# Attention key pages laid out with the head dimension first: no turning of key pages, one ring of key buffers

## The reference, cut to what matters

```
s = einsum('bqngd,bqknd->bqngk', qg, kg) * Dh ** -0.5     # 8 query heads on 2 key heads
s = where(valid, s, -inf);  p = softmax(s)
y = einsum('bqngk,bqknd->bqngd', p, vg)
```

## Time and profile before

| | |
|---|---|
| runs | 1834.33, 1837.55, 1839.07 us, median 1837.55 |
| profiled execution, first to last instruction | 1838.1 us |
| its whole time | not shown apart; its span lies within the three runs' times |
| PE busy | 1747.2 us, 95% |
| DVE, ACT, POOL busy | 979.2, 612.0, 413.3 us |
| instructions | 26511 |

### The profile page before, as it was taken

How to read it: one execution, slowest core, us unless ns; L and a number is a source line. 1 busy time by engine, 2 the same in 40 slices (tenths; PEclk the granted TensorE clock), 3 DMA queues, 4 the chain that set the end, 5 groups by cost and what they waited for, 6 DMA issues and landing times. The chain is left out here.

```text
span 1838.1 us, 26511 instructions
## 1 busy us (share of the span) xinstructions
PE 1747.2 (95%) x9413; PEld 1351.6 (74%) x9413; DVE 979.2 (53%) x2279; ACT 612.0 (33%) x1271; POOL 413.3 (22%) x643
## 2 busy tenths in 40 slices
PE   6999999999999998998999999999999679999999
PEld 5666788777887887886876566887777456777887
DVE  5412644233677555212442568888879665774111
ACT  3110332111122113101211346888745445553010
POOL 4301221100143352000342001211005455420000
PEclk9999999999999999999999999999999899999999
DMA  6433343544556467122222121334344774242231
GB/s 215 131 111 117 120 122 100 162 140 148 181 180 186 128 226 300 76 96 70 82 68 75 47 75 65 117 99 146 126 142 116 252 229 156 90 127 66 105 121 46
DMA packets 134765, 237.10 MB, mean 129 GB/s; under 512 B 28550, under 2 KB 61222, under 8 KB 134634
## 3 DMA queue, kind: packets, MB, share of 16 engines
q1 hardware_dynamic: 111066, 172.48, 29.2%
q0 software_dynamic: 17184, 55.85, 9.6%
q10 hardware_dynamic: 6384, 7.08, 1.1%
HBM read 169.12 MB, written 66.17 MB: 128 GB/s over the span
## 5 line engine op out<-in xcount | busy, mean ns | idle before, releaser
L1282 PE MATMUL ring_acc<-ring_w_hi,layer_xT_hi 128*128 128x512 f32 x640 | 260.8, 407 | 0.2 <-PE all_banks L1432 0.2
L1284 PE MATMUL ring_acc<-ring_w_hi,layer_xT_lo 128*128 128x512 f32 x640 | 249.9, 391 | 0.0
L1283 PE MATMUL ring_acc<-ring_w_lo,layer_xT_hi 128*128 128x512 f32 x640 | 249.7, 390 | 0.0
L2869 PE MATMUL front_acc<-front_w_hi,front_xT_hi 128*128 128x512 f32 x520 | 217.1, 417 | 8.3 <-DVE front_w_lo L3415 6.5
L2871 PE MATMUL front_acc<-front_w_hi,front_xT_lo 128*128 128x512 f32 x520 | 204.5, 393 | 0.0
L2870 PE MATMUL front_acc<-front_w_lo,front_xT_hi 128*128 128x512 f32 x520 | 204.2, 393 | 0.0
L1282 PEld LDWEIGHTS ring_acc<-ring_w_hi,layer_xT_hi 128*128 128x128 f32 x640 | 120.3, 188 | 29.5 <-issue 6.6
L1284 PEld LDWEIGHTS ring_acc<-ring_w_hi,layer_xT_lo 128*128 128x128 f32 x640 | 120.1, 188 | 26.2
L1283 PEld LDWEIGHTS ring_acc<-ring_w_lo,layer_xT_hi 128*128 128x128 f32 x640 | 120.4, 188 | 25.3 <-issue 2.6
L3195 ACT ACTIVATE front_index_rows<-odd_bias,front_candidate,front_minus_sign 128x1024 bf16<-128x1024 f32 (+1 forms) x124 | 132.5, 1075 | 7.2 <-DVE front_candidate L3509 7.2
L2869 PEld LDWEIGHTS front_acc<-front_w_hi,front_xT_hi 128*128 128x128 f32 x520 | 97.9, 188 | 40.3 <-issue 11.8
(11 more groups left out here) (718 smaller groups left out, 3594.6 us busy)
## 6 DMA issues: line engine op xcount, KB each, us to landing
all_w<-in_w_even POOLq DMA_DIRECT2D x80, 256.0 KB, 3.8
h_even<-layer_st SPq DMA_DIRECT2D x79, 256.0 KB, 2.2
all_w<-in_w_odd POOLq DMA_DIRECT2D x61, 256.0 KB, 3.4
h_odd<-front_st SPq DMA_DIRECT2D x55, 256.0 KB, 2.1
layer_scratch<-h_even SPq DMA_DIRECT2D x46, 256.0 KB, 3.0
all_scratch<-in_w_mem SPq DMA_DIRECT2D x32, 256.0 KB, 3.8
all_scratch<-h_even SPq DMA_DIRECT2D x32, 256.0 KB, 3.6
all_scratch<-x SPq DMA_DIRECT2D x14, 512.0 KB, 3.8
```

The lines of the kernel that those rows point to most:

```text
L1282: T.matmul(out[0:rows, :], xh[:, kk, to], wh[:, r, :], start=(kk == 0), stop=False)
L1283: T.matmul(out[0:rows, :], xh[:, kk, to], wl[:, r, :], start=False, stop=False)
L1284: ins = T.matmul(out[0:rows, :], xl[:, kk, to], wh[:, r, :], start=False, stop=(kk == KC - 1))
L2869: T.matmul(out[0:rows, :], xh[:, k, to], wh[:, r, :], start=(k == 0), stop=False, skip_group_check=True)
```

## The change

The host lays the cache out as `cache_attn_kT[layer, page, kv_head, head_dim, position]`, so that a page arrives with the head dimension on the partitions: 128 partitions with 2 runs of 128 positions, 512 bytes each. The transposes, both copies, the ring skT and the semaphores ktr, kca and kcd go. There is one set of key buffers: units 0 and 1 in the four raw tiles (loaded by SP in the front stage, with one DMA for each page and key head, 16 of 64 KB), and eight places for the units from 2 on (`wide`, `place`); units 10 to 15 take the places of units 2 to 7 again and wait for the scores of the group that used them (`keys_free`). Units 2 and 3 are no longer loaded in the front stage. In the back stage step s loads unit s + 1: unit 2 in step 1, unit 3 in step 2, and so on, with AHEAD = 3. The scores wait for their own group's pages.

```diff
@@ layer1_front, SP @@
             def first_keys(u, to, n_pool):
                 for p in range(4):
                     page = sp.value_load(c.page_ids[...], min_val=0, max_val=n_pool - 1)
-                    src = a["cache_attn_k"][0, bass.ds(page, 1)].rearrange("o s h d -> (o s) (h d)")
-                    sp.dma_start(to[p], src).then_inc(kp_in, 16)
+                    src = a["cache_attn_kT"][0, bass.ds(page, 1)].rearrange("o n d s -> d (o n) s")
+                    for n in range(KVH):
+                        sp.dma_start(to[n][:, P * p:P * p + P], src[:, n, :]).then_inc(kp_in, 16)
...
                 sp.wait_ge(vmix, NB)
-                for u in (2, 3):
-                    first_keys(u, [Q[:, EARLY_KEYS + ...] for p in range(4)], n_pool)
+                for _ in range(2):
                     yield
@@ layer1_back @@
+        place = lambda u: u if u < 10 else u - 8
+        wide = {r: (... four places of WH and WL for r in 2 to 9 ...)}
+        keys_of = lambda u, n: c.raw[KVH * u + n] if u < 2 else wide[place(u)][:, n, :]
...
+        def key_page(eng, u, p):
+            at = PAGES * seq_of(u) + 4 * unit(u)[1] + p
+            page = eng.value_load(c.page_ids[0:1, at:at + 1], ...)
+            return a["cache_attn_kT"][0, bass.ds(page, 1)].rearrange("o n d s -> d (o n) s")
+
+        def keys_free(eng, u):
+            if place(u) != u:
+                eng.wait_ge(sc2, place(u) // 4 + 1)
@@ SP @@
             def load_k(u):
-                if u >= KRING:
-                    sp.wait_ge(ktr, 2 * (u - KRING + 1))
+                keys_free(sp, u)
                 for p in range(4 - len(by_pool(u))):
-                    sp.dma_start(kp[r][p], src).then_inc(kp_in[r], 16)
+                    sp.dma_start(wide[place(u)][:, :, P * p:P * p + P], key_page(sp, u, p)).then_inc(kp_in[u // 4], 16)
...
-                for u in range(UNITS + 7):
-                    if u + KRING < UNITS:
-                        load_k(u + KRING)
+                load_k(2)
+                yield
+                for u in range(UNITS + 6):
+                    if u + AHEAD < UNITS:
+                        load_k(u + AHEAD)
@@ POOL: the same for load_last_k @@
@@ PE @@
-            def turned(u):
-                ...
-                for n, (bank, copied) in enumerate(((bankX, kca), (bankZ, kcd))):
-                    pe.wait_ge(copied, u)
-                    for p in range(4):
-                        ins = T.transpose(bank[:, P * p:P * p + P], kp[r][p][:, HD * n:HD * n + HD], c.ident[:, :])
-                    ins.then_inc(ktr, 1)
             def smp_scores(m):
-                pe.wait_ge(kca, 4 * m + 4)
-                pe.wait_ge(kcd, 4 * m + 4)
                 if m == 0:
                     pe.wait_ge(qcp, 6)
+                late = range(max(2, 4 * m), 4 * m + 4)
+                pe.wait_ge(kp_in[m], 16 * sum(4 - len(by_pool(u)) for u in late))
+                pe.wait_ge(kq_in[m], 16 * sum(len(by_pool(u)) for u in late))
                 pe.wait_ge(ye, m)
@@ ACT and DVE: one copy for each unit goes, the steps stay @@
-                    A(skT[u % TRING][:, 0, :], bankX, ACT.Copy).then_inc(kca, 1)
-                        V.tensor_copy(skT[u % TRING][:, 1, :], bankZ).then_inc(kcd, 1)
@@ host @@
+    r["cache_attn_kT"] = turned(f["cache_attn_k"], 0, 1, 3, 4, 2)
```

More of the change, by code:

```diff
@@ L2353, in front_plan @@
     return plan, amid
-EARLY_KEYS = 2640
+MEM_PAGES = 2640
 def layer1_front(nc, c, a, o):
@@ L2434, in layer1_front @@
         qTm = S[:, 4096:5120].rearrange("p (h b q) -> p h b q", h=NH, b=NB)
-        cc = [Q[:, EARLY_KEYS + 1024 * u:EARLY_KEYS + 1024 * u + 1024].rearrange("p (m n) -> p m n", m=MC) for u in range(2)]
+        cc = [Q[:, MEM_PAGES + 1024 * u:MEM_PAGES + 1024 * u + 1024].rearrange("p (m n) -> p m n", m=MC) for u in range(2)]
         mss, mx, tot = ([s.sb(f"{n}{u}", [P, NH]) for u in range(2)] for n in ("mem_rstd", "mem_max", "mem_total"))
@@ L2646, in loads_qk @@
                 sp.dma_start(c.rope[0:SMP, TILES], a["rope"][SEQ:TOK]).then_inc(qk_par, 16)
-                n_pool = a["cache_attn_k"].shape[1]
+                n_pool = a["cache_attn_kT"].shape[1]
                 yield
                 sp.wait_ge(vmix, NB)
-                for u in (2, 3):
-                    first_keys(u, [Q[:, EARLY_KEYS + 1024 * (u - 2) + 256 * p:EARLY_KEYS + 1024 * (u - 2) + 256 * p + 256] for p in range(4)], n_pool)
+                for _ in range(2):
                     yield
@@ L2659, in loads_qk @@
                 for u in range(2):
-                    first_keys(u, [c.key_page(u, p) for p in range(4)], n_pool)
+                    first_keys(u, [c.raw[KVH * u + n] for n in range(KVH)], n_pool)
                 yield
@@ L4108, in load_last_k @@
             def load_last_k(u):
-                r, (gr, hf, _) = u % KRING, unit(u)
-                if u >= KRING:
-                    pool.wait_ge(ktr, 2 * (u - KRING + 1))
+                keys_free(pool, u)
                 for p in by_pool(u):
[L4113 to L4116, removed]
+                    pool.dma_start(wide[place(u)][:, :, P * p:P * p + P], key_page(pool, u, p)).then_inc(kq_in[u // 4], 16)
             def load_v(b, pages):
@@ L4122, in smps @@
             def smps():
-                for u in range(UNITS + 7):
-                    if u + KRING < UNITS:
-                        load_last_k(u + KRING)
+                load_last_k(2)
+                yield
+                for u in range(UNITS + 6):
+                    if u + AHEAD < UNITS:
+                        load_last_k(u + AHEAD)
                     if 12 <= u < 16:
@@ L4198, in smp_scores @@
                         u, e = 4 * m + q, slice(32 * q, 32 * q + 32)
-                        ins = T.matmul(bankY[e, :], qz[:, n, seq_of(u), e], skT[u % TRING][:, n, :], start=(n == 0), stop=(n == 1),
+                        ins = T.matmul(bankY[e, :], qz[:, n, seq_of(u), e], keys_of(u, n), start=(n == 0), stop=(n == 1),
                                        skip_group_check=True)
@@ L4407, in smps @@
             def smps():
-                for u in range(UNITS):
-                    act.wait_ge(ktr, 2 * u + 1)
-                    if u >= TRING:
-                        act.wait_ge(sc2, (u - TRING) // 4 + 1)
-                    A(skT[u % TRING][:, 0, :], bankX, ACT.Copy).then_inc(kca, 1)
+                for _ in range(UNITS):
                     yield
```

45 lines of the change are left out of this document (13 added, 32 removed).

## The result

The changed kernel takes 1840.71 us (median of 19 runs, 1836.37 to 1847.37) against 1837.52 us of the kernel before beside it (19 runs, 1834.07 to 1841.41). The ratio is 1.0020, 95% interval 1.0011 to 1.0029: 3.2 us slower by the medians, 3.7 by the ratio. The loss is just to be told from nothing, and lies inside the 0.3% that the prediction called no change. PE's work fell as the diff says, and the time did not follow.

A forecast was written before the change was run, and what follows sets the result against it. It took a chain of waits to bound the stage around the change, and busy PE from 1514 on. Front +0.2, first scores 0, step 13 +2.5, later steps -2.3 gave +0.4 on 1838.1: 1838.5 us, range 1832.5 to 1844.

The forecast's parts named there:

- six signs of being right: First scores within 1.5 us of 1447.6; step 12 after POOL, 1-2.5 early; third group waits 3+, takes 3.6; product near 1498.
- Front, +0.2: End of front stage: second DMAs at about 0.45 us each, partly covered; between 0 and +0.8 us, taken as +0.2.
- First scores, 0: First group's scores, step 5: page landing and removed turns taken as equal, start 1447.6 as before; 0, kept -1.5 to +2.
- DVE, -1.2: Steps 5 to 7: two turn copies ahead of DVE's sums go, so the sums start earlier; -1.2 us.
- POOL's pow, -0.7: Steps 7 to 9: pow no longer stands behind POOL key pages that wait for a turn; -0.7 us.
- Its issues, 0: POOL's three page issues between pow and its rotation's end: taken as unchanged, 0, with a bound of +1.7 us.
- Step 13, +2.5: Third group's scores: new 3.7 us wait for unit 11's page, issued behind POOL's rotation, then half-clock scores; +2.5 us.
- Steps 13 to 17, -2.3: Second-last scores to the new keys' product: two copies (0.6, 0.7) and a 1.0 us wait go; -2.3 us.
- "And the same at the end", 0: From the product for the new keys at 1497.6 to the kernel's end: the +0.4 us carried on unchanged.
- Late pages: First scores wait 2 us more, three POOL issues double: +3.7 us, 1842; counted within the no-change case, chance 0.66.
- The slower one: Clock stays at half, small products of steps 13 to 18 take twice as long: +8.3 us, 1847; chance 0.19.
- The faster one: Turns were the path: unit 11's page in time, third group's scores 2.9 us early; -6.2 us, 1832; chance 0.15.

The follow-up runs named there:

- e3_front: Changed kernel with one DMA instead of two for each front-stage key page (8 issues, not 16); 1840.1 us against 1839.2 before the change, ratio 1.0004.
- e2_lead: Changed kernel with units 2 and 3 both loaded in the first step and later pages a step earlier (AHEAD = 4); 1839.8 us against 1839.2, ratio 1.0013.
- b5: Changed kernel with 1 KB page runs, lead of four units, first group's scores two steps later, eight identity transposes a step; 1832.2 us against 1837.8 before the change.
- b6: Changed kernel with the first group's scores two steps later and eight identity transposes a step, nothing else; total time not given in the text.
- b3: Changed kernel with 1 KB page runs, lead of four units, first group's scores two steps later; total time not given, front's store to step 20 takes 102.8 us.

## Why the prediction was right, and where its steps were not

The sum said +0.4 us and the runs say +3.3; the time is in the range and in the case that had 0.66. Part of that is luck. The working had step 12 at -1.9 us and it came at +1.7. It had +4.4 from there to the scores' end and that was +1.7. The two errors, 3.6 and 2.7 us, have opposite signs. Of the prediction's six signs of being right only one came true, that step 12 is released by POOL's rotation: the first scores start at 1450.39 and not within 1.5 us of 1447.6, step 12 is late and not early, the third group waits 1.0 us and not 3 and takes 1.92 us and not 3.6, and the product for the new keys starts at 1500.25 and not near 1498. None of its signs of being wrong came true either. Its steps, in its order:

*Front, +0.2.* Measured +1.1 (16.91 to 18.05 from F), the upper end of the scatter. A second DMA costs 0.62 us (13.62 less 8.64 over 8), not 0.45, 5.0 us in all, and the cover of half a microsecond was gone. My own upper bound of 0.8 was passed. e3_front gives it all back.

*First scores, 0.* Measured +2.0, of which 1.1 is the front and 0.8 the pages. As a size this is inside -1.5 to +2. As a reading it was the weakest step: I asked whether turns and pages would end at the same time, and they nearly do, but not what stood behind the answer. Before, the page that PE waited for ahead of these scores was unit 4's, whose turn stands ahead of them in step 5 (L4187, 3.09 us of waiting until 1445.67); the group's own pages were there. Afterwards it is a page of the group itself. Without the pages' wait these scores start 5.0 us ahead of the kernel before (F + 27.7), and with the group two steps later step 20 moves by 5.6. The gain of the change was there, and this wait ate it. The packets' price that I took from the earlier trace rows, +41%, lies above what landings show, 5.2 against 4.1 us, +27%; the +9% estimated from the Trainium skill ("DMA: Bandwidth & Descriptors", section "Why small descriptors are slow (HBM only)") lies below.

*DVE, -1.2.* From the first scores to the sums: 10.86 before, 10.23 after, -0.6. The copies went, but ACT's squares are at 1459.33, behind a copy that waits for transposes at half clock (1.12 us), and the sums follow them.

*POOL's pow, -0.7.* From the sums to pow 2.37 before, 1.79 after: -0.6, right. *Its issues, 0.* They cost +0.5 for three (0.77, 0.75, 0.72 against 0.62, 0.58, 0.54), and one gap ahead of an issue is 0.5 longer: from pow to PE's step 12 16.4 before and 17.4 after. Inside the bound of 1.7. So step 12 is at +1.7 from F, not -1.9.

*Step 13, +2.5.* The new wait is there, for the reason named: unit 11's page is issued 1.33 us behind the rotation's end, and e2_lead, which issues it earlier, takes it away. It is 1.0 us and not 3.7, since the page landed in 2.9 us and PE needed 3.25 us for step 12, at half clock, where I gave it 1.6. The scores then ran at the full clock in 1.92 us, not in 3.6. From step 12 to the scores' end: 4.5 before, 6.2 after, +1.7; I had +4.4, hidden in part by the lead of 1.9 that did not come.

*Steps 13 to 17, -2.3.* To the product for the new keys it is -1.6 (15.87 before, 14.30 after). So the product starts at +1.85 from F where the sum had +0.4.

*"And the same at the end", 0.* This is the term that was missing: step 20 is at +3.3 and not at +1.85. The chain of waits goes from the product over the job behind it on PE to DVE's mask, ACT's exponentials of the samples and PE's next jobs; POOL is not in it, and PE has no idle time ahead of tile 4's first transposes in either kernel. PE's pieces of that job, before and then after:

```profile
1501.18 0.55 PE all_banks L4291 x4
1501.73 0.33 PE all_banks L4282 x3
1502.06 0.66 PE back_s L4268 x2
```

```profile
1503.88 0.96 PE all_banks L4276 x4
1504.84 0.64 PE all_banks L4267 x3
1505.48 1.29 PE back_s L4253 x2
```

They take 1.54 us before and 2.89 after, +1.35: the same work, nearly all of it at half clock right behind a product at full clock. From the mask on it is +0.1. The prediction had priced half clock only up to the product, and there it took 0.

*The rivals.* Late pages was the nearest: pages and POOL's issues, priced at 1842, 1842.3 profiled. The slower one, half clock to the end, is true for most of the time up to step 12 and in single stretches later (0.62 in 1494 to 1498, and the job behind the product, +1.35 us), not at the product for the new keys, which takes 3.63 us as before. By the rule of the Trainium skill ("TensorE: Matmul & The Clock Gate", section "HAM oscillation — how this bites in real kernels") bursts between waits are throttled anew; the trace agrees, with 0.50 in 1474 to 1482 after 1.92 us scores at the full clock. The faster one, 1832, asked for the page of unit 11 in time and 1 us at the first scores. b5, where both waits are gone, has its number (1832.2), but not its way: it needed the later group and the added transposes, and e2_lead, with that page in time, gained only 2.1 us.

## What to carry to other kernels

When a change takes work out from in front of a wait, ask what that wait will be once the work is gone: here half of the first group's pages (units 2 and 3) had been loaded a stage ahead, and the change took away the turns and put these pages' landing in front of the scores. (Loading them ahead again was not tried.) An operation of an in-order engine that needs a transfer belongs as late as its reader allows, not where its predecessor stood; two steps were worth 5.6 us and no instruction. And follow the path past the last operation that the change touches: work that is the same in both kernels can run at another clock, here for 1.35 of the 3.3 us lost.

## What the runs showed of the hardware

- A second DMA for each of eight pages costs SP 0.62 us each in this pair of kernels (13.62 against 8.64 us), and 0.5 to 0.63 over all of them (13.2 to 13.7 against 8.6 to 9.2).
- A 128 KB page of 512-byte runs is issued by POOL in 0.72 us and one of 1 KB runs in 0.54, and both follow each other every 1.15 us: the price shows only where computation stands behind the issue.
- Two edits that give 0.2 and 0.5 us alone gave 2.6 together. With the page late the third group waits (b6, 0.77 us) and the clock is down behind the product (4.65 us to ACT's exponentials in place of 3.70); with the page there but no added transposes it is down there too (b3, 5.16 us).
- The same pair of multiplications on POOL (128x1024 f32) takes 3.16 to 3.27 us, or 3.63 to 3.85 where DVE's operation on `odd_bias` for the ties lies inside it.
- Eight transposes of the identity a step (1.04 us at the full clock) brought step 20 forward: 2.6 us on the changed kernel, 1.2 of it in POOL's stretch, and 2.1 on b3, all of it behind the third group.
